# Two unused buffers of 64 and 96 bytes shift the other buffers of an fp32 transformer kernel in SBUF

## The reference

```python
def swiglu(h, w_gate, w_up, w_down):
    return (jax.nn.silu(h @ w_gate) * (h @ w_up)) @ w_down
...
        hn = rms_norm(h, norm_mix_g[l])
        proj = jnp.einsum('bsd,de->bse', hn, w_in[l])
...
        up = jax.nn.relu(jnp.einsum('bsd,df->bsf', hn, w_mlp_up[l]))
        h = h + jnp.einsum('bsf,fd->bsd', up * up, w_mlp_down[l])
```

## Time and profile before

| | us |
|---|---|
| median of 3 runs (lowest, highest) | 3443.09 (3441.97, 3445.67) |
| span of the profiled execution, first to last instruction | 3439.6 |
| TensorE busy with matmuls | 3350.8 |
| VectorE busy | 1958.2 |
| ScalarE busy | 1336.1 |
| GpSimd (POOL) busy | 216.9 |

### The profile page before, as it was taken

One profiled execution on the slowest core, in us unless ns is written; L12 is line 12 of the kernel. 1 busy time (PEld: TensorE's weight loads), 2 busy tenths in 40 slices (PEclk: granted clock), 3 DMA queues, 4 the chain that ended last, 5 costly groups with the idle time before them and its releaser, 6 DMA issues.

```text
span 3439.6 us, 42270 instructions
## 1 busy us (share of the span) xinstructions
PE 3350.8 (97%) x15606; PEld 2748.9 (80%) x15606; DVE 1958.2 (57%) x2680; ACT 1336.1 (39%) x1896; POOL 216.9 (6%) x174
## 2 busy tenths in 40 slices
PE   7999999999999999999999999999999999999999
PEld 5878777888888888877778888888888777888887
DVE  4677766564446544578754544464446985454444
ACT  4455434432224332445644322342224565442223
POOL 1000000000000000026100000000000550000000
PEclk9999999999999999999999999999999999999999
DMA  4333332233333333322221333333333222123332
GB/s 130 99 86 86 98 92 89 87 113 98 98 98 90 94 98 98 92 86 78 82 80 56 97 98 98 89 107 95 96 89 94 86 86 74 62 85 95 93 95 86
DMA packets 426827, 314.26 MB, mean 91 GB/s; under 512 B 17512, under 2 KB 423456, under 8 KB 426672
## 3 DMA queue, kind: packets, MB, share of 16 engines
q1 hardware_dynamic: 422880, 302.13, 29.3%
q0 software_dynamic: 2896, 8.49, 0.8%
q10 hardware_dynamic: 896, 1.54, 0.1%
HBM read 309.99 MB, written 2.13 MB: 91 GB/s over the span
## 4 chain that ended last, share of the span: by engine, by line
PE 87%; DVE 8%; ACT 2%; issue 2%; DMA 0%; ACTq 0%; DVEq 0%
PE G L722 76%; PE G L888 2%; DVE w_lo L1978 1%; PE G L869 1%; DVE arena L1827 1%; ACT w_hi L1246 1%; DVE small L1826 1%; PE B L711 1%; PE G L661 1%; PE B L640 1%; PE B L612 1%; PE G L907 1%; PE G L922 1%; PE B L572 0%; PE B L989 0%
## 5 line engine op out<-in xcount | busy, mean ns | idle before, releaser
L1246 ACT ACTIVATE w_hi<-raw 128x1024 fp32r<-128x1024 f32 x579 | 613.6, 1060 | 1470.2 <-PE G L722 1411.8
L1978 DVE TENSOR_TENSOR w_lo<-raw,w_hi 128x1024 fp32r<-128x1024 f32 x580 | 718.8, 1239 | 673.7 <-ACT w_hi L1246 671.1
L722 PE MATMUL G<-y_hi,w_hi 128*128 128x512 f32 x2320 | 915.3, 395 | 9.1 <-DVE w_lo L1978 8.3
L722 PE MATMUL G<-y_hi,w_lo 128*128 128x512 f32 x2320 | 903.5, 389 | 0.0
L722 PE MATMUL G<-y_lo,w_hi 128*128 128x512 f32 x2320 | 903.0, 389 | 0.0
L722 PE MATMUL G<-xn_hi,w_hi 128*128 128x512 f32 x1808 | 710.6, 393 | 9.5 <-DVE w_lo L1978 5.0
L722 PE MATMUL G<-xn_hi,w_lo 128*128 128x512 f32 x1808 | 704.1, 389 | 0.0
L722 PE MATMUL G<-xn_lo,w_hi 128*128 128x512 f32 x1808 | 703.8, 389 | 0.0
L722 PEld LDWEIGHTS G<-y_hi,w_hi 128*128 128x128 f32 x2320 | 435.5, 188 | 111.4 <-issue 16.5
L722 PEld LDWEIGHTS G<-y_lo,w_hi 128*128 128x128 f32 x2320 | 435.6, 188 | 93.3 <-issue 4.6
L722 PEld LDWEIGHTS G<-y_hi,w_lo 128*128 128x128 f32 x2320 | 435.4, 188 | 91.2
(11 more groups left out here) (431 smaller groups left out, 3116.4 us busy)
## 6 DMA issues: line engine op xcount, KB each, us to landing
raw<-in_w_in SPq DMA_DIRECT2D x128, 512.0 KB, 4.4
raw<-in_ffn_w_gate SPq DMA_DIRECT2D x88, 512.0 KB, 4.0
raw<-in_ffn_w_up SPq DMA_DIRECT2D x88, 512.0 KB, 5.2
raw<-in_ffn_w_down SPq DMA_DIRECT2D x64, 512.0 KB, 4.3
raw<-in_w_mlp_up SPq DMA_DIRECT2D x32, 512.0 KB, 4.6
raw<-in_w_mlp_down SPq DMA_DIRECT2D x32, 512.0 KB, 4.3
raw<-in_xa_wkv SPq DMA_DIRECT2D x32, 512.0 KB, 4.5
raw<-in_w_out SPq DMA_DIRECT2D x24, 512.0 KB, 4.3
```

What stands on the lines that cost most here:

```text
L722: m = pe.matmul(bank[:, 0:n], a[:, k, kt, :], b[:, kt * S:kt * S + n], start=(kt == tiles[0] and t == 0), stop=(kt == tiles[-1] and t == 2))
L1246: act.activation(w_hi[:, k], raw[:, 1 - q, :, k * P:(k + 1) * P], ACT.Copy).then_inc(s_whi, 1)
L1978: dve.tensor_tensor(w_lo[:, k], raw[:, 1 - q, :, k * P:(k + 1) * P], w_hi[:, k].bitcast(F32), ALU.subtract)\
```

## The change

Two buffers are reserved that nothing writes or reads. The first, 16 floats (64 bytes per partition), stands in front of `raw`. The second, 24 floats (96 bytes), stands in front of `y_hi`.

```diff
+        sb("before_weights", [P, 16])
         raw = sb("raw", [P, 2, KT, 256])
         w_hi = sb("w_hi", [P, 2, KT, P], F32R)
         w_lo = sb("w_lo", [P, 2, KT, P], F32R)
         xn_hi = sb("xn_hi", [P, KT * S], F32R)
         xn_lo = sb("xn_lo", [P, KT * S], F32R)
+        sb("before_inner", [P, 24])
         y_hi = sb("y_hi", [P, KT * S], F32R)
         y_lo = sb("y_lo", [P, KT * S], F32R)
```

## The result

The changed kernel takes 3484.8 us (median of 4 runs, 3483.5 to 3487.6) against 3442.5 (4 runs, 3441.5 to 3445.7): a ratio of 1.012, 95% interval 1.0108 to 1.0132. It is slower by 42.3 us, far outside the range of 3436 to 3451, in a direction that had a chance of 0.08.

The account below looks back on a forecast made before the run. TensorE was taken as the bound, busy 3350.8 of 3439.6 us. Every term of the change was put at zero, so the span stayed 3439.6 us and the forecast median 3443.1 us, range 3436 to 3451.

Parts of the forecast that it names:

- The transfer of rows 12: Weight transfer into raw: issued at 1147.68, lands about 5.2 us later, with 7.9 us of slack; forecast cost zero.
- the 0.5 us more: Landing of weights in raw: 22 beats in place of 20 per 512-byte row, estimated 10% or 0.5 us, covered by slack.
- The covers: Slack hiding delays outside TensorE: 3.1 us at a panel's split, 7.9 us for weight transfers; both terms put at zero.
- The price of 7.6 us for each nanosecond: One nanosecond more on each y product was to cost 7632 * 0.001 = 7.6 us.
- The section on what would show it: Signs expected in the changed profile: y steps 227 for no change, 228 or more beside xn 227 for (a), 226 or less (b).
- rival (a): y's odd start makes float32r streams touch 33 64-byte pieces, not 32: 51 us slower, 3494 us (half a piece 3468); chance 0.07.
- Does the phase between two streams matter at all?: Step on TensorE's moving stream against its weights: answered no on three observations, so y's 96 bytes out of step cost zero.
- The fixed part: About 13 ns that every float32r matmul was taken to carry whatever its length; losing it all would gain 99 us.
- The neighbouring argument: Engines starting at independent times already average over hundreds of phases, so buffer offsets between them cost TensorE nothing: zero.
- The bound: Cost of y's odd start, from plain float32 matmuls in arena: at most 0.003 us a step, 23 us in all.
- Rival (b): Common start was bad; 96 bytes between y and weights removes some fixed part: 25 us gained (3418), at most 99 (3344); chance 0.06.

## Why the prediction was wrong

**What held.** TensorE sets the time, no instruction moved, and the prices of VectorE, ScalarE and the loads stayed as read. The transfer of rows 12 still lands after 5.2 us (median), so the 0.5 us more that were estimated for the new start of `raw` do not show. The covers held as well: the loss is in TensorE's steps. The price of 7.6 us for each nanosecond is a little high: 6.3 ns give 48 by it, 42.3 were measured, because the 384 short products did not slow down at this distance and TensorE's waits became shorter. The section on what would show it named the sign, a y step above 227 beside xn steps of 227, but called it proof of rival (a). That was wrong: the sign came, and (a) is not the cause.

**The step that failed** is "Does the phase between two streams matter at all?", which I answered with no on three observations. The term was put at zero and measured 6.3 ns on each y product (233.3 against 227.0), some 42 us.

1. "The distance between the two streams takes many values already." It does, but 4096k + 512kt and 2048kt are all multiples of 256, and the effect repeats after 256. In all 12,384 products of L722 the trace held one single value. Many samples of one case say nothing on another.
2. "They sweep at different speeds, and a start offset only shifts the moment at which they are level." The sweeps are tied together in every step: the load of the next tile starts some 3 ns after the matmul it runs beside, thousands of times alike. An offset between the two is therefore not averaged as it is between engines that start independently. That this tie is why the distance counts is my reading, no run shows it. The neighbouring argument, for VectorE and ScalarE against TensorE, did hold: while one of them is busy the steps are longer by 0.5 ns at most, in both kernels.
3. "The fixed part is the same 13 ns when the moving stream is half as long, so it isn't made of meetings." The fixed part was compared at one distance only, 0. At 96 bytes the short steps keep their mean of 119 to 120 ns while the long ones lose 6.3, and at 192 the short ones fall to 115.5 while the long ones rise to 233.3. What is equal at distance 0 is not equal elsewhere, so the comparison said nothing on the others.

A matmul of the kernel before and the load that runs beside it, for the second point:

```profile
1150.17 0.39 PE L722 MATMUL G<-xn_hi,w_lo 128*128 128x512 f32 x1
1150.18 0.19 PEld L722 LDWEIGHTS G<-xn_hi,w_hi 128*128 128x128 f32 x1
```

**The bound** of a small loss was too small in consequence. 0.003 us came from plain float32 matmuls in arena (the four records there are two matmuls of the kernel, each in two records); the float32r ones lost 0.0063 us. Those rows bound the price of an odd start, which is indeed nothing, and not the price of a distance. They differ from the products of y in type as well, and whether plain float32 matmuls mind the distance no run shows, since both operands always lie in arena.

**Rival (a)** gave 51 us, and 42.3 were measured, but its mechanism is refuted: with every stream at an odd start the time was 3443.0, and in the run with 32 bytes twice the oddly placed xn was the fast one. The size agreed by chance. Rival (b) saw that y and the weights leave their common phase and had the sign wrong for products of 512 columns, where the common phase is the best one tried; those of 256 columns do gain at some distances, though not at 96 bytes, and nearly all the time is in the long ones. That all buffers had sat at one phase was in the table of addresses; I used it for hope of a gain, and priced leaving it at nothing in the forecast.

**How far the sum closes.** The extra of a step times 7248 y and 5712 xn products gives about 82 us for distances of 224 and 288, and one run gave 71. Compared step by step with the kernel before, that trace has 79.3 us more in the y and xn steps that were under 260 ns. The longer ones, with a wait in them, have 6.0 us less: TensorE is slower, and so it waits less for the others, which are not. The other stages have 2.1 us less, which is within what they differ by from run to run. Together that is 71.2 of the 71.1 us by which the spans differ. With 64 bytes on y the same product gives 14.6 and 16.0 were measured.

**What stays open.** The runs show that the distance modulo 256 bytes sets the step, and that the number of columns and the width of the stationary tile change how. What in the memory or in TensorE's reading does this, whether it is the load that meets the moving stream, why steps with no odd pair in them are delayed as well, why 64 bytes cost a third of 32, and why the short products gain where the long ones lose, they do not show. Five of the twelve experiments, among them those of the repetition at 288 and of the half load, rest on a single execution each; the steps are read over thousands of products in it, the time only once. Distances under 16 bytes were not tried.

## What to carry to other kernels

Where TensorE is the bound, look at the addresses of its moving and stationary operands modulo 256, not only at the order of the work: in this kernel a small buffer reserved between the two costs 0.5 to 1.2% with one activation pair out of step and 2.1 to 2.2% with both, on the products that read across it and on no others. It was the products of 512 columns that lost; those of 256 columns gained a little at most distances, so a kernel of short products has to be measured. If a small buffer has to be added to a kernel like this one, put it in front of all of them or behind, or round it to 256 bytes. And before a trace is taken as evidence that some quantity does not matter, check that the quantity varies in it.

## What the runs showed of the hardware

- Products of 512 float32r columns step by 226.7 ns when moving and stationary operands are a multiple of 256 bytes apart, and by 228.9 to 234.3 ns at the other distances tried. Moving both operands together (from 128 to 160 past a multiple of 512) made no difference.
- The steps of 256 float32r columns have a mean of 119.1 ns at distances of 0 and 256 and 119.5 at 96, and are shorter at others: 117.2 at 32, 116.9 at 64, 115.5 at 192.
- The steps of plain float32 matmuls in arena, whose two operands moved together, stayed at 215 to 217 ns.
- A stationary load of 64 columns lasts 135 ns and one of 128 columns 188. With products narrowed to 64 stationary columns the steps at distance 0 were slower, 229.6 in place of 226.7.
- VectorE and ScalarE took the same times in the changed kernel, to within 5 ns (1060 ns for the split of ScalarE, 692 for `h<-G,h`, as before). While one of them was busy, TensorE's steps were longer by 0.5 ns at most (227.1 and 226.7 for y in the kernel before).
